# A two-block layer on one Trainium2 core: state space outputs with channels on partitions, the order of the delta walk, and how the substitution is shared out

## What is computed

```python
q, k, v, z_a, b_a, a_a, z_s, x_s, b_s, c_s, dt_s = jnp.split(h @ w_in, offsets, axis=-1)
o_a = gdn_chunked(q, k, v, g, beta)                 # 8 heads of 128: the delta rule, chunk by chunk
o_a = rms_norm(o_a, gdn_norm_w) * silu(z_a)
y = ssd_chunked(xs_, dt, a_neg, bm, cm)             # 2 groups x 8 heads of 64 channels, state 128
y = y + ssd_d * xs_
y = rms_norm(y * silu(z_s), ssd_norm_w)
mix = jnp.concatenate([o_a, o_s], axis=-1) @ w_out
```

```python
y_diag = einsum("bgls,bghls,bsghp->blghp", cb, lmat, xdt)   # (C B^T * decay) times x dt
y_off  = einsum("blgn,bghpn,bghl->blghp", c, state, exp(acs))
state  = state * exp(acs[-1]) + einsum("bsgn,bghs,bsghp->bghpn", b, decay, xdt)
```

## Time and profile before

| | |
|---|---|
| median of 3 runs | 1627.12 us (1625.51 to 1627.35) |
| profiled execution | 1626.75 us, span of its instructions 1624.9 us |
| TensorE busy | 1586.6 us, 98% of the span |
| VectorE busy | 931.4 us, 57% |
| ScalarE busy | 671.5 us, 41% |
| GpSimd busy | 170.3 us, 10% |
| mean DMA rate | 110 GB/s |
| mean granted TensorE clock | 0.997 of 2.4 GHz |

### The profile page before, as it was taken

One profiled execution on the slowest core, in us unless ns is written; L12 is line 12 of the kernel. 1 busy time (PEld: TensorE's weight loads), 2 busy tenths in 40 slices (PEclk: granted clock), 3 DMA queues, 4 the chain that ended last, 5 costly groups with the idle time before them and its releaser, 6 DMA issues.

```text
span 1624.9 us, 21269 instructions
## 1 busy us (share of the span) xinstructions
PE 1586.6 (98%) x8221; PEld 1306.4 (80%) x8221; DVE 931.4 (57%) x1390; ACT 671.5 (41%) x1159; POOL 170.3 (10%) x191
## 2 busy tenths in 40 slices
PE   7999999999999999999999999999999999999998
PEld 6877878788787877788888788778778888888886
DVE  5678858856636677766434547555556533333334
ACT  5464456554334333344323454444444422232321
POOL 2011215510001000000000133311000000000000
PEclk9999999999999999999999999999999999999999
DMA  6354224220164886632323133122224233323232
GB/s 197 91 118 121 74 78 104 78 67 27 63 222 136 292 270 225 208 113 84 120 91 129 34 102 85 54 71 65 65 78 130 65 103 90 103 91 103 91 101 67
DMA packets 195400, 179.08 MB, mean 110 GB/s; under 512 B 5982, under 2 KB 175021, under 8 KB 192244
## 3 DMA queue, kind: packets, MB, share of 16 engines
q1 hardware_dynamic: 191888, 169.56, 34.2%
q10 hardware_dynamic: 2276, 6.95, 1.3%
q0 software_dynamic: 1152, 1.44, 0.5%
HBM read 173.58 MB, written 4.58 MB: 110 GB/s over the span
## 4 chain that ended last, share of the span: by engine, by line
PE 90%; DVE 5%; ACT 2%; DMA 2%; issue 1%; POOL 0%; SPq 0%; DVEq 0%; ACTq 0%; POOLq 0%
PE acc L657 17%; PE acc L658 16%; PE acc L659 16%; PE acc L698 7%; PE acc L700 7%; PE acc L699 7%; PE acc L1195 2%; PE acc L1197 2%; PE acc L713 2%; PE acc L711 2%; PE acc L712 2%; PE acc L1196 2%; DMA early<-decay_rows 1%; PE acc L1339 1%; DVE w_low L2090 1%
## 5 line engine op out<-in xcount | busy, mean ns | idle before, releaser
L2090 DVE TENSOR_TENSOR w_low<-w_raw,w_high 128x1024 fp32r<-128x1024 f32 x230 | 285.0, 1240 | 529.8 <-ACT w_high L1418 529.4
L1418 ACT ACTIVATE w_high<-w_raw 128x1024 fp32r<-128x1024 f32 x224 | 237.3, 1059 | 633.8 <-PE acc L659 380.4
L657 PE MATMUL acc<-h_high,w_high 128*128 128x512 f32 (+1 forms) x1248 | 487.7, 391 | 8.3 <-DVE w_low L2090 2.8
L659 PE MATMUL acc<-h_high,w_low 128*128 128x512 f32 (+1 forms) x1248 | 480.1, 385 | 0.0
L658 PE MATMUL acc<-h_low,w_high 128*128 128x512 f32 (+1 forms) x1248 | 479.9, 385 | 0.0
L657 PEld LDWEIGHTS acc<-h_high,w_high 128*128 128x128 f32 x1248 | 235.3, 189 | 68.4 <-issue 17.9
L659 PEld LDWEIGHTS acc<-h_high,w_low 128*128 128x128 f32 x1248 | 235.1, 188 | 46.9
L658 PEld LDWEIGHTS acc<-h_low,w_high 128*128 128x128 f32 x1248 | 235.3, 189 | 45.3 <-issue 1.2
L698 PE MATMUL acc<-w_high,act_high 128*128 128x512 f32 x496 | 193.4, 390 | 2.8 <-DVE arena L2810 1.5
L700 PE MATMUL acc<-w_high,act_low 128*128 128x512 f32 x496 | 193.0, 389 | 0.0
L699 PE MATMUL acc<-w_low,act_high 128*128 128x512 f32 x496 | 193.0, 389 | 0.0
(11 more groups left out here) (388 smaller groups left out, 1942.5 us busy)
## 6 DMA issues: line engine op xcount, KB each, us to landing
w_raw<-w_in SPq DMA_DIRECT2D x68, 512.0 KB, 3.9
w_raw<-w_mlp SPq DMA_DIRECT2D x64, 512.0 KB, 3.8
w_raw<-w_up SPq DMA_DIRECT2D x44, 512.0 KB, 4.0
arena<-w_ada SPq DMA_DIRECT2D x13, 1024.0 KB, 8.0
w_raw<-w_out SPq DMA_DIRECT2D x24, 512.0 KB, 3.3
early<-w_ada SPq DMA_DIRECT2D x11, 1024.0 KB, 6.5
w_raw<-w_down SPq DMA_DIRECT2D x22, 512.0 KB, 3.3
w_raw<-w_branch_gate SPq DMA_DIRECT2D x16, 512.0 KB, 3.9
```

What stands on the lines that cost most here:

```text
L657: pe.matmul(out_, wh, xh, start=start, stop=False)
L659: return pe.matmul(out_, wl, xh, start=False, stop=stop)
L1418: f(WH[:, off % 2, :], RAW[:, off % 4, :], ACT.Copy).then_inc(sem("w_high"), 1)
L2090: tt(WL[:, off % 2, :], RAW[:, off % 4, :], WH[:, off % 2, :].bitcast(F32), ALU.subtract).then_inc(sem("w_low"), 1)
```

## The change

It has four parts.

1. **State space outputs with channels on partitions.** For y_diag the turned x (64 columns a head) becomes the stationary operand and the head's weights move over 128 columns. Even heads write PSUM partitions 0 to 63, odd ones 64 to 127. For y_off the state is stationary in four blocks a group and C moves over 128 columns. The sum needs no turning: `y_turn` and `y_out` go. The decay exp(acs), until now a scale per partition, has to vary along the free dimension: `faded_rows(c)` fetches it for c = 1 to 3 with two DMAs (512 KB in all) on SyncE's queue, and ScalarE exponentiates it. `skip_d` becomes a scale per partition (`skip_of`), used in eight 128-column instructions of `y_sum`.
2. **The walk.** `late_k` moves from VectorE to ScalarE (8 instructions instead of 2). VectorE's order becomes `less_state`, `solved`, `o_sum(c - 1)`, `stated`, `o_normed(c - 1)`, `gated(11 + c)`.
3. **The walk's end.** `gated(15)` is split in halves on TensorE with the turns of chunks 0 to 2 between, and `o_gated` runs in another order.
4. **The substitution.** The steps between `gated(i)` are shared out as 8, 5, 5, 6, 7 instead of 7, 6, 6, 6, 6.

```diff
+            def faded_rows(c):
+                if c > 2:
+                    sp.wait_ge(sem("s_y"), 2 * c - 2)
+                else:
+                    sp.wait_ge(sem("rows_stored"), 16)
+                for e in range(2):
+                    src = bass.AP(gcum.tensor, (8 + e) * T + c * P, [[0, 64], [2 * T, 8], [1, P]])
+                    sp.dma_start(A[64 * e:64 * e + 64, ER_[c % 2]:ER_[c % 2] + 1024].rearrange("p (h t) -> p h t", t=P),
+                                 src).then_inc(sem(f"s_fade_in{c % 2}"), 16)
...
                 if i == 7:
                     state_rows(1)
+                    faded_rows(1)
...
                 if i == 1:
                     state_rows(2)
+                    faded_rows(2)
                 if i == 5:
                     state_rows(3)
+                if i == 6:
+                    faded_rows(3)
...
                 if c:
-                    pe.wait_ge(sem("y_turned_out"), 2 * c)
-                pe.wait_ge(sem("s_x_out"), c + 1)
+                    pe.wait_ge(sem("s_y"), 2 * c)
+                pe.wait_ge(sem("s_x"), c + 1)
...
                 for g in range(2):
-                    for h in range(8):
-                        m = pe.matmul(PS[:, 3 + 2 * g, h * PD:(h + 1) * PD], weights(c, g)[:, h * P:(h + 1) * P],
-                                      arena(TT_ + (8 * g + h) * PD, PD), start=True, stop=True)
-                    if c:
-                        m = pe.matmul(PS[:, 6 + g, :], FT[:, C0 + g, tc], arena(SS_ + g * 512, 512),
-                                      start=True, stop=True)
+                    for i in range(4):
+                        for e in range(2):
+                            h = 2 * i + e
+                            m = pe.matmul(PS[64 * e:64 * e + 64, 3 + 2 * g, i * P:(i + 1) * P],
+                                          arena(TT_ + (8 * g + h) * PD, PD), weights(c, g)[:, h * P:(h + 1) * P],
+                                          start=True, stop=True)
+                for g in range(2 if c else 0):
+                    for i in range(4):
+                        m = pe.matmul(PS[:, 6 + g, i * P:(i + 1) * P], arena(SS_ + g * 512 + i * P, P),
+                                      FT[:, C0 + g, tc], start=True, stop=True)
...
-                if c:
-                    y_turn(c - 1)
                 state_turn(c)
...
-            def o_turn(c):
-                pe.wait_ge(sem("d_o"), 2 * NT)
+            def o_turn(c, q):
                 if c == NT - 1:
-                    pe.wait_ge(sem("z_silu"), 16)
+                    pe.wait_ge(sem("z_silu"), 15 + q)
+                else:
+                    pe.wait_ge(sem("d_o"), 2 * NT)
+                pe.wait_ge(sem("d_normed"), 2 * c + q + 1)
...
-            gated(15)
-            for c in range(NT):
-                o_turn(c)
-            row_block(0, WO_N, 0, WO_A, True, lambda t: pe.wait_ge(sem("d_gated"), 2 * ((t + 3) % 4) + 2),
+            gated(15, [0])
+            for q in range(2):
+                for c in range(NT - 1):
+                    o_turn(c, q)
+            gated(15, [1])
+            for q in range(2):
+                o_turn(NT - 1, q)
+            row_block(0, WO_N, 0, WO_A, True, lambda t: pe.wait_ge(sem("d_gated"), (t + 3) % 4 + 4 + (t == 0)),
...
+                if c:
+                    act.wait_ge(sem(f"s_fade_in{c % 2}"), 32 if c < 3 else 64)
+                    f(arena(ER_[c % 2], 1024), arena(ER_[c % 2], 1024), ACT.Exp).then_inc(sem("s_fade"), 1)
                 act.preload_act_table_set("silu_and_others")
...
+            def late_k(c, q):
+                if c:
+                    act.wait_ge(sem("d_out"), 2 * c - 1 + q)
+                for h in range(4 * q, 4 * q + 4):
+                    m = f(KB[:, h, :], PS[:, 2 + 3 * q, (h % 4) * P:(h % 4 + 1) * P], ACT.Copy, scale=kds[:, c, h:h + 1])
+                m.then_inc(sem("d_kd"), 1)
...
-            gated(15)
+            used(0, Z_N + 15)
+            f(z_gate(7), PS[:, 1, :], ACT.Silu).then_inc(sem("z_silu"), 1)
+            split(0, Z_N + 17)
...
-            def y_sum(c, g):
-                y, xd = arena(VN_ + g * 512, 8, PD), arena(PP_ + g * 512, 8, PD)
-                if c == 0:
-                    tt(y, whole(3 + 2 * g), xd, ALU.add).then_inc(sem("s_y"), 1)
-                    return
-                step(tt(y, whole(3 + 2 * g), xd, ALU.add))
-                step(tt(xd, whole(6 + g), rate(ecum, c, g), ALU.mult))
-                tt(y, y, xd, ALU.add).then_inc(sem("s_y"), 1)
+            def y_sum(c):
+                tc = slice(c * P, (c + 1) * P)
+                y = arena(YS_, 2, T)
+                if c:
+                    dve.wait_ge(sem("s_fade"), c)
+                    step(tt(y, PS[:, 6:8, :], arena(ER_[c % 2], 2, T), ALU.mult))
+                    step(tt(y, y, PS[:, 3:7:2, :], ALU.add))
+                for i in range(8):
+                    old = arena(YS_ + i * P, P) if c else PS[:, 3 + i // 4 * 2, i % 4 * P:(i % 4 + 1) * P]
+                    m = stt(FT[:, X0 + i, tc], FT[:, X0 + i, tc], skip_of[:, i:i + 1], old, ALU.mult, ALU.add)
+                    if i % 4 == 3:
+                        m.then_inc(sem("s_y"), 1)
...
-                tt(arena(PP_, HS, PD), xt, skip_d.unsqueeze(2).to_broadcast([P, HS, PD]), ALU.mult)\
-                    .then_inc(sem("s_x_out"), 1)
...
-            eliminate(31, 24)
+            eliminate(31, 23)
             gated(2)
-            eliminate(24, 18)
+            eliminate(23, 18)
             gated(3)
-            eliminate(18, 12)
+            eliminate(18, 13)
             gated(4)
-            eliminate(12, 6)
+            eliminate(13, 7)
             gated(5)
-            eliminate(6, 0)
+            eliminate(7, 0)
...
             for c in range(1, NT):
-                if c < NT - 1:
-                    for q in range(2):
-                        late_k(c, q)
                 for q in range(2):
                     less_state(c, q)
                 for q in range(2):
-                    o_normed(c - 1, q)
+                    solved(c, q)
                 for q in range(2):
-                    solved(c, q)
+                    o_sum(c - 1, q)
                 if c == NT - 1:
                     for j in range(2):
                         act_split(0, j, WO_A, mixed)
                 for q in range(2):
                     stated(c, q)
-                gated(11 + c)
                 for q in range(2):
-                    o_sum(c, q)
-            gated(15)
+                    o_normed(c - 1, q)
+                if c < NT - 1:
+                    gated(11 + c)
+            for q in range(2):
+                o_sum(NT - 1, q)
+            gated(14)
             for q in range(2):
                 o_normed(NT - 1, q)
-            for c in range(NT):
-                for q in range(2):
-                    o_gated(c, q)
+            for c in range(NT - 1):
+                o_gated(c, 0)
+            for c in range(NT - 1):
+                o_gated(c, 1)
+            for q in range(2):
+                o_gated(NT - 1, q)
+            gated(15)
```

More of the change, by code:

```diff
@@ L118 @@
 M_ = CH * T
-QE_, R_, TT_, NM_, PP_, VN_, SS_ = (M_ + 1024 * i for i in (0, 1, 2, 3, 4, 6, 8))
+QE_, R_, TT_, NM_, YS_, SS_ = (M_ + 1024 * i for i in (0, 1, 2, 3, 6, 8))
+ER_ = (M_ + 4096, M_ + 5120)
 GQ_, GN_, ZA_ = M_, M_ + 4096, M_ + 8192
@@ L296, in program @@
         skip_d = small(HS)
+        skip_of = small(8)
         modT = small(NADA, 2)
@@ L835, in state_out @@
                 m.then_inc(sem("s_sum"), 1)
-            def y_turn(c):
-                for g in range(2):
-                    pe.wait_ge(sem("s_y"), 2 * c + 2)
-                    for i in range(4):
-                        m = pe.transpose(PS[:, 5 + g, i * P:(i + 1) * P],
-                                         arena(VN_ + g * 512 + i * P, P), IDN)
-                    m.then_inc(sem("y_turned"), 1)
             for c in range(NT):
@@ L1012, in outputs @@
                 m.then_inc(sem("d_out"), 1)
-            def o_turn(c):
-                pe.wait_ge(sem("d_o"), 2 * NT)
+            def o_turn(c, q):
                 if c == NT - 1:
-                    pe.wait_ge(sem("z_silu"), 16)
-                for q in range(2):
-                    pe.wait_ge(sem("d_normed"), 2 * c + q + 1)
-                    for h in range(4 * q, 4 * q + 4):
-                        m = pe.transpose(PS[:, (2 * c + 2) % 8 + q, (h % 4) * P:(h % 4 + 1) * P], GQ[:, 8 * c + h, :],
-                                         IDN)
-                    m.then_inc(sem("d_o_turned"), 1)
+                    pe.wait_ge(sem("z_silu"), 15 + q)
[3 more added lines that the diff above has]
+                for h in range(4 * q, 4 * q + 4):
+                    m = pe.transpose(PS[:, (2 * c + 2) % 8 + q, (h % 4) * P:(h % 4 + 1) * P], GQ[:, 8 * c + h, :], IDN)
+                m.then_inc(sem("d_o_turned"), 1)
             conv(28)
             conv(29)
-            y_turn(NT - 1)
+            pe.wait_ge(sem("s_y"), 2 * NT)
```

(24 more changed lines are left out.)

16 lines of the change are left out of this document (4 added, 12 removed).

## The result

The changed kernel takes 1617.37 us (median of 4 runs, 1616.55 to 1618.89) where the kernel before took 1627.23 in the same set of runs: a ratio of 0.9947, 95% interval 0.9935 to 0.9959. The medians are 9.9 us apart where 8.2 were forecast; by the interval the gain lies between 6.7 and 10.6 us. In the four later sets of runs the kernel before took 1624.8 to 1625.4 us, some 2 us less than here, so the 9.9 is rather too high. The profiled execution took 1616.78 us, with a span of 1615.0.

A forecast was written before the change was run, and what follows sets the result against it. TensorE, busy 98% of the span with 90% of the chain, bounds the kernel. Terms -0.9 + 3.2 + 2.15 + 3.7 = 8.2 us, so 1627.1 - 8.2 = 1618.9 us; range 1615.4 to 1624.2.

The forecast's parts named there:

- y_diag: State space stage: column halves overlap twofold, 1.93 us a chunk instead of 3.46, saving 1.5 us a chunk.
- Rival A: y_diag: the column halves don't overlap, 3.7 us a chunk; total 1624.1 us; chance 0.11.
- B: y_diag's 32 records: weight loads no longer hide behind their streams; 7.1 us slower, 1634.2 us; chance 0.05.
- Chunk 0: End of chunk 0: longer y_sum(0) delays chunk 1's turn, 0.9 us lost; TensorE's gap grows to about 5.2 us.
- Chunks 1 to 3: State space stage: 1.6 us won in each of chunks 1 and 2, 2.15 us in chunk 3.
- Substitution: New sharing of the substitution's steps: no gain, with 0.4 us on either side.
- Walk, chunk 2: Before solve of chunk 2: without o_sum(1) and late_k in front, less_state ends in time; 1.5 us won.
- Walk, chunk 3: Before solve of chunk 3: two o_sum no longer in front, solve right after q_state, 0.9 us earlier.
- End: Walk's end: with the new order the output product starts near 429.4 instead of 430.72; 1.3 us won.
- C: Chunk 0: the first faded_rows pair delays state_rows(1), which VectorE waits for; total 1622.4 us; chance 0.11.
- D: Walk: the waits only move, less_state waits for scaled v and solve for it; total 1622.6 us; chance 0.08.
- E: Chunk 0: TensorE's slow stretch falls into the longer gap; 1617.3 us, or 1616.5 with cheaper y_sum(0); chance 0.05.

The follow-up runs named there:

- state_only: The kernel before with only the new state space outputs; walk, its end and substitution as before: 1621.46 us, ratio 0.9983.
- end_undone: The changed kernel with the walk's last gate block undivided and its turns and gates in the old order: 1617.19 us, ratio 0.9950 to the kernel before.
- k_on_vector: The changed kernel with the walk's late_k back on VectorE, ahead of less_state: 1618.69 us, ratio 0.9967 to the kernel before.
- halves_in_turn: The changed kernel with y_diag doing a group's four even heads, then its four odd ones, instead of alternating: 1619.69 us, ratio 0.9968 to the kernel before.
- fade_first: The changed kernel with SyncE issuing the copies faded_rows(1) ahead of the critical state_rows(1), not behind: 1623.03 us, ratio 0.9988 to the kernel before.
- subst_only: The kernel before with only the substitution's steps shared out as 8, 5, 5, 6, 7: 1625.03 us, ratio 0.9999.
- state_first: The changed kernel with VectorE making the new state ahead of y_sum's eight 128-column instructions: 1613.40 us, ratio 0.9929 to the kernel before.

## Why the prediction was right, and where it was not

**y_diag**: forecast 1.93 us a chunk, measured 1.89. The twofold overlap and a cheap entry hold: half of 32 x 0.111 is 1.78, and the rest is 0.11. Rival A is out, and so is B. The answer for L844 in chunk 2 (durations min/median/max in ns, first and last start in us) shows the weight loads overlapping the streams:

```profile
L844 PEld LDWEIGHTS acc<-arena x32: 132/137/137, 176.6 to 178.2; 128*64 128x64 f32 x32
L844 PE MATMUL acc<-arena x32: 272/273/323, 176.6 to 178.3; 128*64 128x128 f32 x32
```

The loads alone, one after the other, would be 32 x 0.137 = 4.4 us; they start within 1.6. By the rule of the Trainium skill (TensorE: Matmul & The Clock Gate, The mechanism) a load hides only when its row group differs. These have all rows in common and hide; the measurement decides.

**y_off**: 150.63 - 148.74 = 1.89 for 1.82: nothing, as said.

**Chunk 0**: forecast 0.9 us lost up to the turn of chunk 1, 0.24 measured. The mechanism is as forecast: the turn starts 1.32 us later, of which 0.88 is the longer `y_sum` and 0.44 the later landing of the decays. The size in this trace is luck. The slow stretch at 14 us made the stage start 1.08 us late, and the critical copy was issued about as much later (107.82 for 106.78), but it took 9.4 us instead of 10.0, so the wait took in 0.64 of the delay. In the other traces with the change's order in chunk 0, y_diag to the turn takes 14.89 (state_only), 14.69 (end_undone), 14.75 (k_on_vector) and 14.68 us (halves_in_turn), for 13.77 before: 0.9 to 1.1 lost. The gap is 4.64 where I had about 5.2; in the first three of these it is 5.3 to 5.5, and 4.7 in halves_in_turn, where y_diag is longer.

**Chunks 1 to 3**: 1.55 each and 2.05, for 1.6 and 2.15. The wait before the turn shows as 0.5, not 0.8. It costs 0.8 all the same: the turn starts 0.70 us later behind the state's product than before, and what follows it takes 0.14 longer. y_off cost 0.06.

**Substitution**: forecast 0, measured 0.2 alone and 0.48 here, just past my 0.4. I looked at the one wait over 1 us and missed the second:

```profile
319.63 0.47 PE L657 MATMUL acc<-h_high,w_high 128*128 128x512 f32 x1 [0.38 <-DVE w_low L2090]
```

It goes, as `gated(5)` comes a step earlier. That the end is set by VectorE's 31 steps was not so before, where TensorE did not wait at L916; with the new share it does, 0.44 us.

**Walk, chunk 2**: 1.53 for 1.5. The place was right, but of the two things that I put in front of `less_state` only `o_sum` mattered, as k_on_vector shows.

**Walk, chunk 3**: 1.28 for 0.9, and this is the term that was mis-sized. The wait for `less_state` gave 0.75 of the forecast 0.9. Before, `q_state` of chunk 3 also waited for scaled v, in a row that I had not read:

```profile
407.56 2.19 PE L985 MATMUL acc<-early,arena 128*128 128x128 f32 x16 [0.34 <-ACT early L1713]
```

0.27 of that went. And 0.26 went behind `solve` of chunk 2, which no longer follows a wait: a row that does is longer, 2.19 against 1.95.

**End**: 1.41 for 1.3, right by size and wrong by cause. I gave it to the split of the last block. end_undone shows that VectorE's order won 1.85 and the split gave 0.44 back.

**The total**: the stages add up to 9.9 where I had 8.2. Of the 1.7 more, 0.4 lies outside what was changed and 0.5 in chunk 0, where one quick copy hid the loss; both are luck. The substitution gave 0.5, and `solve` of chunk 3 0.4.

**Rivals**: C is out, since the differences started at 117.23 (116.8 in state_only, end_undone and halves_in_turn) and fade_first shows how a delay would have looked. D is out: `solve` follows `q_state` at once. E did not happen in chunk 0: the slow stretch lay behind the gap again.

## What to carry to other kernels

Where an array is used in halves, look at whether the saving arrives: here three of four chunks kept it, and the first gave it up to the order of another engine's queue, in which eight instructions needed by nobody for a long time stood ahead of one that everybody waited for. Mend that order first and price the change against the mended kernel. When stages and medians disagree by more than 1 us, look for stretches of lower clock before you believe either.

## What the runs showed of the hardware

- **Two half-width tiles of float32 run beside each other**, 0.059 us a record (1.89 / 32) against about 0.11 for one at a time, and the overlap reaches across runs of eight records (0.078 a record over all in halves_in_turn, 2.50 / 32).
- **Copies on SyncE's queue were served in order**: 0.5 MB ahead of the critical copy moved the differences from 117.23 to 121.84, and behind it the copy took 9.4 to 10.3 us for 10.0 without it.
- **A slow stretch of TensorE's clock has a fixed price here.** In all 14 profiles the loss before the last 10 us is 0, 1.7, 3.4 or 5.1 us. In chunk 0, behind gaps of 1.6, 4.6, 4.7 and 5.4 us the traces have one such unit, behind 5.3 and 5.5 us two, and behind 10.6 us three, most of it inside the gap. Behind 1.9 us (subst_only) and 3.1 us (state_first) they have none, so a gap of this size brings it only sometimes. In subst_only the turn of chunk 1 to y_diag took 17.95 us where before took 19.58.

The granted clock (last but two) in stretches of 2 us in fade_first, with TensorE idle from 121.2 to 131.7, shows it falling while the engine waits and not when it starts again:

```profile
122.00:124.00 2.00, 0.00 (x0) 0.00 (x0) 2.00 (x12) 0.47 (x1) 0.00 (x0) 1.00 0.29 88
124.00:126.00 2.00, 0.00 (x0) 0.00 (x0) 2.00 (x7) 1.49 (x2) 0.00 (x0) 0.86 0.00 0
126.00:128.00 2.00, 0.00 (x0) 0.00 (x0) 1.93 (x4) 1.98 (x3) 0.00 (x0) 0.50 0.16 33
132.00:134.00 2.00, 2.00 (x11) 2.00 (x11) 1.97 (x3) 0.00 (x0) 0.00 (x0) 0.50 0.96 157
136.00:138.00 2.00, 2.00 (x11) 1.61 (x10) 0.24 (x1) 0.00 (x0) 1.86 (x2) 1.00 0.90 80
```
